# Eight tiles of each down-projection take seven block products instead of seven tiles, and part of the weight sums is made by DMA

## The reference

```
def squared_relu_mlp(n, w_up, w_down):
    return jnp.square(jax.nn.relu(n @ w_up)) @ w_down      # 1024 -> 4096 -> 1024

h = h + squared_relu_mlp(rmsnorm(h, g_ffn[layer]), w_up[layer], w_down[layer])   # layer 0 and 1
```

## Time and profile before

| what | us |
|---|---|
| median of three runs | 946.07 (945.78 to 946.14) |
| profiled execution, device time | 946.75 |
| its span | 944.8 |
| TensorE busy in the span | 935.6 |
| VectorE busy | 712.6 |
| ScalarE busy | 595.3 |
| GpSimd busy | 36.2 |

### The profile page before, as it was taken

How to read it: one execution, slowest core, us unless ns; L and a number is a source line. 1 busy time by engine, 2 the same in 40 slices (tenths; PEclk the granted TensorE clock), 3 DMA queues, 4 the chain that set the end, 5 groups by cost and what they waited for, 6 DMA issues and landing times.

```text
span 944.8 us, 14583 instructions
## 1 busy us (share of the span) xinstructions
PE 935.6 (99%) x5944; PEld 832.5 (88%) x5944; DVE 712.6 (75%) x1037; ACT 595.3 (63%) x869; POOL 36.2 (4%) x15
## 2 busy tenths in 40 slices
PE   8999999999999999999999999999999999999997
PEld 7888888888888888888888888999999999999886
DVE  4997747777988867747777988876468789898643
ACT  7676548888655658838888655734555596555532
POOL 0011250000000000020000000000000000000000
PEclk9999999999999999999999999999999999999999
DMA  8554235555565552535554565454544436555541
GB/s 300 222 183 173 91 134 179 183 200 197 181 220 192 178 209 91 178 136 182 191 207 179 183 218 205 163 191 166 179 165 161 166 134 246 179 179 184 193 158 44
DMA packets 25345, 168.22 MB, mean 178 GB/s; under 512 B 2816, under 2 KB 3904, under 8 KB 5568
## 3 DMA queue, kind: packets, MB, share of 16 engines
q1 hardware_dynamic: 24848, 166.84, 49.5%
q10 hardware_dynamic: 432, 0.46, 0.2%
HBM read 166.24 MB, written 1.05 MB: 177 GB/s over the span
## 4 chain that ended last, share of the span: by engine, by line
PE 94%; DVE 3%; ACT 1%; DMA 1%; issue 1%; SPq 0%; DVEq 0%
PE bank L724 23%; PE bank L725 23%; PE bank L726 23%; PE bank L833 12%; PE bank L837 6%; PE bank L752 1%; DMA raw<-w_stream 1%; DVE wlo L1997 0%; PE bank L887 0%; PE bank L1106 0%; PE bank L891 0%; PE bank L895 0%; PE bank L1240 0%; PE bank L1132 0%; PE bank L1114 0%
## 5 line engine op out<-in xcount | busy, mean ns | idle before, releaser
L1997 DVE TENSOR_TENSOR wlo<-raw,whi 128x2048 fp32r<-128x2048 f32 (+2 forms) x133 | 296.8, 2232 | 131.2 <-ACT whi L1340 131.0
L1340 ACT ACTIVATE whi<-raw 128x2048 fp32r<-128x2048 f32 (+1 forms) x139 | 264.7, 1905 | 100.2 <-PE bank L726 97.7
L833 PE MATMUL bank<-nhl,whi 128*128 128x512 f32 x512 | 124.0, 392 | 0.0
L833 PEld LDWEIGHTS bank<-nhl,whi 128*128 128x128 f32 x512 | 94.0, 188 | 18.8 <-issue 0.7
L724 PE MATMUL bank<-mhi,whi 128*128 128x258 f32 x384 | 108.5, 282 | 0.1
L725 PE MATMUL bank<-mlo,whi 128*128 128x258 f32 x384 | 108.3, 282 | 0.0
L726 PE MATMUL bank<-mhi,wlo 128*128 128x258 f32 x384 | 108.2, 282 | 0.0
L724 PE MATMUL bank<-nhl,whi 128*128 128x258 f32 (+3 forms) x320 | 92.2, 288 | 0.0
L725 PE MATMUL bank<-nhl,whi 128*128 128x258 f32 (+3 forms) x320 | 91.4, 286 | 0.0
L726 PE MATMUL bank<-nhl,wlo 128*128 128x258 f32 (+3 forms) x320 | 90.5, 283 | 0.0
L724 PEld LDWEIGHTS bank<-mhi,whi 128*128 128x128 f32 x384 | 72.5, 189 | 0.4 <-issue 0.2
(11 more groups left out here) (389 smaller groups left out, 1914.3 us busy)
## 6 DMA issues: line engine op xcount, KB each, us to landing
raw<-w_stream SPq DMA_DIRECT2D x154, 1024.0 KB, 4.8
h<-x_rows SPq DMA_DIRECT2D x4, 256.0 KB, 5.1
raw<-w_stream SPq DMA_DIRECT2D x2, 512.0 KB, 6.7
cst<-consts SPq DMA_DIRECT2D x1, 832.0 KB, 6.3
e<-g_post SPq DMA_DIRECT2D x1, 512.0 KB, 6.7
out_rows<-e SPq DMA_DIRECT2D x2, 256.0 KB, 2.0
raw<-w_stream SPq DMA_DIRECT2D x1, 352.0 KB, 10.0
vec<-vectors SPq DMA_DIRECT2D x1, 258.5 KB, 9.5
```

The source lines that it names most:

```text
L833: return pe.matmul(us[c].t[:, :], w[:, k, c * P:c * P + P].hi, nboth[:, k, :], start=k == 0, stop=k == 7)
L1340: act.activation(whi[j][:, 0:n], raw[j][:, 0:n], ACT.Copy).then_inc(s_hi.up(i))
L1997: dve.tensor_tensor(wlo[j][:, 0:m], raw[j][:, 0:m], whi[j][:, 0:m].bitcast(F32), ALU.subtract).then_inc(s_lod.up(i))
```

## The change

SEVEN becomes (2, 4, 5, 7, 8, 10, 11, 13): eight tiles for each layer instead of seven, from tile 4 on two of three. The signs of the scheme change so that the first two of the four weight sums are b12 + b11 and b12 + b22. These two are no longer made by VectorE from `raw`. SP issues two transfers of 256 KB, each of which brings b12 from HBM to one half of a buffer `T13` (`right_block`), and when both have landed, GpSimd issues a transfer of 512 KB that adds b11 and b22 to it (`block_sums`, with `accum_op=ALU.add`). There are two buffers T13, used in turn; the first lies where constants of the first block were, the second where `TX[0]` was. VectorE keeps the other two sums, in `T24`. The tile itself is still brought whole to its slot `raw`.

```diff
-SEVEN = (2, 4, 6, 8, 10, 12, 13)
+SEVEN = (2, 4, 5, 7, 8, 10, 11, 13)
...
-        TX = [at(f"tr{i}", 1024, o_nhl + 4096 * i) for i in range(2)]
+        o_inval = CST["inval"][0]
+        T13 = [cst[:, o_inval:o_inval + 1024], at("tr0", 1024, o_nhl)]
+        T24 = at("tr1", 1024, o_nhl + 4096)
...
+        def fill(l, q):
+            return len(SEVEN[q % 2::2]) * l + q // 2 + 1
+
+        def t13_ready(l, q):
+            return s_t13[q % 2], 16 * fill(l, q)
+
+        def t_sums(l, q):
+            return T13[q % 2], T24
...
             def combined_hi(l, it):
                 q = SEVEN.index(it)
                 for part in range(2):
-                    on.wait_ge(*s_ts.at(l, q, part))
+                    on.wait_ge(*(s_ts.at(l, q) if part else t13_ready(l, q)))
...
             def combined(l, it):
...
                 on.wait_ge(s_raw[i % NSLOT], 16 * (i // NSLOT + 1))
+                on.wait_ge(*t13_ready(l, q))
                 if q:
                     on.wait_ge(*s_tlo.at(l, q - 1, 1))
-                dve.tensor_tensor(TX[0].rearrange("p (k n) -> p k n", k=2), right, above, ALU.subtract).then_inc(s_ts.up(l, q, 0))
-                on.wait_ge(*s_ts.at(l, q, 0))
-                dve.tensor_tensor(TX[1][:, 0:512], r[:, 1536:2048], TX[0][:, 0:512], ALU.subtract).then_inc(own.up())
+                dve.tensor_tensor(T24[:, 0:512], r[:, 1536:2048], t1, ALU.add).then_inc(own.up())
                 on.wait_ge(*own.last())
-                dve.tensor_tensor(TX[1][:, 512:1024], r[:, 1024:1536], TX[1][:, 0:512], ALU.subtract).then_inc(s_ts.up(l, q, 1))
+                dve.tensor_tensor(T24[:, 512:1024], r[:, 1024:1536], T24[:, 0:512], ALU.add).then_inc(s_ts.up(l, q))
...
         def gpsimd_program(pool):
...
+            def block_sums(l, q):
+                t = t_sums(l, q)[0].rearrange("p (k n) -> p k n", k=2)
+                i = DOWN[l] + SEVEN[q]
+                corner = W[starts[i]:starts[i + 1]].rearrange("(p k n) -> p k n", p=P, k=4)[:, 0:4:3, :]
+                on.wait_ge(s_t12[q % 2], 32 * fill(l, q))
+                pool.dma_start(t, corner, accum_op=ALU.add).then_inc(s_t13[q % 2], 16)
+
             for i in range(2, NTILE):
                 j, m, n = i % NSLOT, cuts[i], sizes[i]
+                if seven_at(i):
+                    block_sums(*seven_at(i))
...
+            def right_block(l, q):
+                t = t_sums(l, q)[0].rearrange("p (k n) -> p k n", k=2)
+                i = DOWN[l] + SEVEN[q]
+                b = W[starts[i]:starts[i + 1]].rearrange("(p n) -> p n", p=P)
+                if q < 2:
+                    on.wait_ge(*use["up", l, 15 * q, q].done())
+                else:
+                    on.wait_ge(*s_ts.at(l, q - 2))
+                    on.wait_ge(*s_tlo.at(l, q - 2, 0))
+                for k in range(2):
+                    sp.dma_start(t[:, k, :], b[:, 512:1024]).then_inc(s_t12[q % 2], 16)
...
+                if i - 1 in (DOWN[0] + SEVEN[1], DOWN[1] + SEVEN[1]):
+                    right_block(*seven_at(i - 1))
+                if seven_at(i) and seven_at(i)[1] != 1:
+                    right_block(*seven_at(i))
```

More of the change, by code:

```diff
@@ L586, in block_kernel @@
         ASP = [Pair(at(f"ash{i}", 512, o, F32R), at(f"asl{i}", 512, o + 2048, F32R)).view("p (i n) -> p i n", i=4) for i, o in enumerate(o_sums)]
-        ASP = [ASP + [f.view("p (m n) -> p m n", m=16)[:, 2:10:2, P:2 * P]] for f in FFP]
+        ASP = [ASP + [f.view("p (m n) -> p m n", m=16)[:, m:m + 12:3, P:2 * P] for m in (2, 4)] for f in FFP]
         AS4 = AS.rearrange("p (i n) -> p i n", i=4)
@@ L682, in block_kernel @@
         s_as, s_ashi, s_aslo = (sig(n, grid(2, len(SEVEN))) for n in ("as", "ashi", "aslo"))
-        s_ts, s_thi, s_tlo = (sig(n, grid(2, len(SEVEN), 2)) for n in ("ts", "thi", "tlo"))
+        s_ts = sig("ts", grid(2, len(SEVEN)))
+        s_thi, s_tlo = (sig(n, grid(2, len(SEVEN), 2)) for n in ("thi", "tlo"))
+        s_t12, s_t13 = ([sem(f"s_{n}_{i}") for i in range(2)] for n in ("t12", "t13"))
+        def fill(l, q):
[4 more added lines that the diff above has]
+            return T13[q % 2], T24
         s_ex = sig("ex", range(2))
@@ L1349, in combined_hi @@
                 for part in range(2):
-                    on.wait_ge(*s_ts.at(l, q, part))
+                    on.wait_ge(*(s_ts.at(l, q) if part else t13_ready(l, q)))
                     if q:
                         on.wait_ge(*use["st", l, 3 - part].done(q - 1))
-                    act.activation(TH[part], TX[part], ACT.Copy).then_inc(s_thi.up(l, q, part))
+                    act.activation(TH[part], t_sums(l, q)[part], ACT.Copy).then_inc(s_thi.up(l, q, part))
             def down_hi(l, it):
@@ L2324, in combined @@
                 q, i = SEVEN.index(it), DOWN[l] + it
-                r = raw[i % NSLOT]
-                right, above = r.rearrange("p (k c n) -> p k c n", k=2, c=2)[:, :, 1, :], r[:, 0:1024].rearrange("p (k n) -> p k n", k=2)
+                r, t1 = raw[i % NSLOT], t_sums(l, q)[0][:, 0:512]
                 on.wait_ge(s_raw[i % NSLOT], 16 * (i // NSLOT + 1))
+                on.wait_ge(*t13_ready(l, q))
                 if q:
                     on.wait_ge(*s_tlo.at(l, q - 1, 1))
-                dve.tensor_tensor(TX[0].rearrange("p (k n) -> p k n", k=2), right, above, ALU.subtract).then_inc(s_ts.up(l, q, 0))
-                on.wait_ge(*s_ts.at(l, q, 0))
-                dve.tensor_tensor(TX[1][:, 0:512], r[:, 1536:2048], TX[0][:, 0:512], ALU.subtract).then_inc(own.up())
+                dve.tensor_tensor(T24[:, 0:512], r[:, 1536:2048], t1, ALU.add).then_inc(own.up())
                 on.wait_ge(*own.last())
-                dve.tensor_tensor(TX[1][:, 512:1024], r[:, 1024:1536], TX[1][:, 0:512], ALU.subtract).then_inc(s_ts.up(l, q, 1))
+                dve.tensor_tensor(T24[:, 512:1024], r[:, 1024:1536], T24[:, 0:512], ALU.add).then_inc(s_ts.up(l, q))
             def combined_lo(l, it):
@@ L2341, in combined_lo @@
                     on.wait_ge(*s_thi.at(l, q, part))
-                    dve.tensor_tensor(TL[part], TX[part], TH[part].bitcast(F32), ALU.subtract).then_inc(s_tlo.up(l, q, part))
+                    dve.tensor_tensor(TL[part], t_sums(l, q)[part], TH[part].bitcast(F32), ALU.subtract).then_inc(s_tlo.up(l, q, part))
             def down_lo(l, it):
@@ L2373, in seven_2 @@
                 on.wait_ge(*p7.gone())
-                dve.tensor_tensor(EX[3], EX[1], p5.t[:, :], ALU.add).then_inc(s_ex.up(l))
-                dve.tensor_tensor(EX[0], EX[2], p5.t[:, :], ALU.add).then_inc(p5.free)
+                dve.tensor_tensor(EX[3], p5.t[:, :], EX[1], ALU.subtract).then_inc(s_ex.up(l))
+                dve.tensor_tensor(EX[0], p5.t[:, :], EX[2], ALU.subtract).then_inc(p5.free)
                 on.wait_ge(*s_ex.at(l))
@@ L2398, in row_sums @@
                     on.wait_ge(*s_ffsq.at(l, m))
-                    dve.tensor_tensor(s1, a21, a22, ALU.add).then_inc(own.up())
+                    dve.tensor_tensor(s1, a21, a22, ALU.subtract).then_inc(own.up())
                     on.wait_ge(*own.last())
@@ L2403, in row_sums @@
                     on.wait_ge(own.sem, own.n - 1)
-                    dve.tensor_tensor(s4, a12, s2, ALU.subtract).then_inc(s_as.up(l, q))
+                    dve.tensor_tensor(s4, a12, s2, ALU.add).then_inc(s_as.up(l, q))
                 def row_sums_lo(m):
@@ L2408, in row_sums_lo @@
                     on.wait_ge(*s_ashi.at(l, q))
+                    on.wait_ge(*s_fflo.at(l, m))
                     s = ASP[l][q]
@@ L2869, in stage @@
                         if seven_at(i - NSLOT):
-                            on.wait_ge(*s_ts.at(*seven_at(i - NSLOT), 1))
+                            on.wait_ge(*s_ts.at(*seven_at(i - NSLOT)))
                         if cuts[i - NSLOT]:
```

## The result

| | before | after |
|---|---|---|
| median, us | 946.0 (945.51 to 946.38, 6 runs) | 989.23 (987.78 to 994.53, 6 runs) |
| ratio | | 1.047 (95% interval 1.0454 to 1.0487) |

The account below looks back on a forecast made before the run. TensorE, busy 935.6 of 944.8 us, was taken to bound the kernel. The median 946.07, less 1.36 of matmuls, plus 5.8 of waits on the transfer chain, gave 950.5 us; range 944.3 to 957.3.

Parts of the forecast that it names:

- The direct gain: TensorE in the down-projections: one block product less in each of two layers saves 1.36 us, 0.14%.
- The loop: Tile 8 reuses tile 5's buffer T13, so its sums wait for VectorE's rest, b12 twice and GpSimd's adding transfer.
- C: Time from the rest of tile 5 to the landed sums of tile 8: 10.0 us, ends 7.5 and 14.7.
- limit of 8.2 us: Longest C for tile 11 without a TensorE wait if tile 8 was late: 14.97 - 6.8 = 8.2 us.
- The 8.9 for tile 8: Longest C for tile 8 without a TensorE wait: 14.97 + 2.0 - 6.8 - 1.3 = 8.9 us.
- upper end of 14.7: The high end given for C, the time from tile 5's rest to tile 8's landed sums: 14.7 us.
- b12 twice: SP's two b12 transfers, 512 KB, priced between 64 KB at 2.4 and 1024 KB at 4.8 us: 3.6 us.
- adding transfer behind it: GpSimd's 512 KB adding transfer after its issue: 5.3 us, between 3.5 and 7.1.
- The windows of the other pairs: Time for the chains of other tiles: 11.6 us for tile 5, 11 to 13 us for tiles 7, 10 and 13.
- the forecast's own formula: TensorE's wait per layer is C - 8.9 at tile 8 plus C - 8.2 at tile 11: 2.9 us, 5.8 in two.
- rival 2: DMA engines become the bound, 15.7 to 17.0 us per three tiles if adding costs twice: 958.5 us, chance 0.22.
- Rival 1: The transfer chain is short enough (C at 8.2) that TensorE has no wait: 944.7 us, chance 0.36.

Follow-up runs that it names:

- experiment 4: Kernel before with only the new SEVEN tile numbers; VectorE makes all four weight sums, no transfers added: 947.64 us, ratio 1.0017.
- 12: Changed kernel, but SP issues tiles 5, 8 and 11 only when the same tile's adding transfer has landed: 1007.54 us (one run).
- experiment 8: experiment 4 plus all the change's transfers, in one series from GpSimd's queue into unread buffers, awaited once per layer: 997.65 us, ratio 1.0541.
- experiment 3: Changed kernel with own buffers for the first two sums of tiles 8, 10, 11 and 13: 966.21 us, ratio 1.0219.
- 1: Changed kernel with the adding left out of GpSimd's transfer, which only copies b11 and b22: 969.22 us (one run).
- 9: Changed kernel with tiles 3 to 14 of each down-projection issued as four 256 KB pieces in 2 KB rows: 979.66 us, ratio 1.0361.
- 14: experiment 3 with tiles 3 to 14 of each down-projection issued as four 256 KB pieces in 2 KB rows: 958.22 us, ratio 1.0134.
- experiment 5: Changed kernel, but VectorE makes the first two sums of tiles 5, 8 and 11; the other five tiles use transfers: 986.6 us, ratio 1.0435.

## Why the prediction was wrong

**The direct gain, 1.36 us.** The matmuls went. In experiment 4, where no transfer disturbs, the time still rose by 1.6 us: VectorE has no gap left in that form, with three instructions for the sums of a tile. With the change's two sums the forecast had 13.8 of 14.97 us for VectorE; the durations are in the trace as taken (0.69 each, `tl` 1.22), so nothing speaks against this step, but it never came to decide.

**The loop.** The mechanism is the forecast's: VectorE's first sum waits for GpSimd's transfer, TensorE for what VectorE does behind it, and a round takes C + 6.8 us (6.5 measured behind the wait, 282.20 to 288.70). The rounds bear out its limit of 8.2 us. The 8.9 for tile 8 took tile 5 to be in time, which it was not. TensorE's waits show at the first products of the tile itself, which need its `lo` (the row at 285.50), not at the first matmul on `th`, as `lo` is queued behind the same wait.

**C = 10.0: the term that failed.** Measured 16.5 for tile 8 and 17.3 for tile 11, over even the forecast's upper end of 14.7 for it. The prediction's own sign of being wrong, an adding transfer that lands over 7 us, is what came.

| term | forecast | after (tile 8) | no plain tile beside it (12, tile 8) |
|---|---|---|---|
| SP's wake | 0.1 | 0.07 | |
| b12 twice | 3.6 | 6.1 | 5.9 |
| GpSimd's issue | 1.0 | 1.2 | 1.2 |
| adding transfer behind it | 5.3 | 9.1 | 4.75 |
| C | 10.0 | 16.5 | 11.9 |

Two terms are off, for two reasons. The b12 pair was priced by size, between 64 KB at 2.4 us and 1024 KB at 4.8. But it took 6.1 us in the kernel after, where nothing else moved from 266 to 270 us, and 5.0 at the end of experiment 8: more than a tile of 1 MB. It is two transfers in rows of 2 KB, cut out of rows of 8 KB; which of the two makes it slow, the rows or the number, no run tells. The adding transfer alone was priced well (4.75, and up to 6.0 in the other places of 12, against 5.3); beside the tiles it takes half as much again to twice that. The forecast took the crowd for a part of it only. In fact the two tiles behind `right_block` begin to move when b12 is in, together with it.

**The windows of the other pairs, 11.6 us and more.** They were called safe, and at C = 10 they are. Tile 5's chain took 259.20 - 240.28 = 18.9 us, and that is the 6 us ahead of the first round.

**From C to the time.** Put into the forecast's own formula, 16.5 - 8.9, 17.3 - 8.2 and 18.9 - 11.6 are 24.0 us in a layer, 48.0 in two; with the gain of 1.36, 992.7 us against 989.2. So the formula holds within 3.5 us and its input was wrong. The forecast let C into the time four times (two waits in two layers); with tile 5's wait it is six. The range reached to C = 11.7 only, though the text had 14.7 as the upper end. By that end alone the formula gives 2 x (29.4 - 17.1 + 3.1) = 30.8 and 975.5 us: a range that takes in the bounds of the unknown costs, as it should, would still have missed, by 14 us and not by 32. The range also left out 958.5, the time of its own rival 2, which had a chance of 0.22. A slip without weight: at C = 11.2 the formula gives 955.3, not 955.1.

**Rival 2, the DMA engines.** Its budget (15.7 to 17.0 us for a round) is near the 17.2 from the shares, but in the kernel after, the engines have a share of 0.80 from 252 to 284 us: the loop ends later. With the loop cut they are full (1.03 in experiment 3). Its time of 958.5 is 8 under the 966.2 of experiment 3.

**Rival 1, the chain closes.** Refuted: even with no plain tile beside it a chain took 11.7 to 13.1 us (8 and 12). The estimate from the Trainium skill (DMA: Bandwidth & Descriptors, Anatomy of one DMA), 3.2 us for 512 KB from GpSimd's queue, is under all that was measured: a plain one took 4.3 and 6.8 us (medians of the two buffers in 1), an adding one 5.9 to 7.2 with the engines to itself. No run has a plain one alone. On adding, the rule of the Trainium skill (the same page, Rules for kernel authors: the accumulate reads its destination) agrees with the doubled packets and engine time. That a DMA engine takes its queues in turns by packets (the Trainium skill, the same page, Queues, rings and completion order) agrees in direction with 9 and 14. No run here shows the turns themselves.

**What stays open.** How the 20 us of experiment 3 divide between full engines and turns: the adding is worth 13.9 of them and the small rows 8, which is more than 20 together, so the two overlap. Why b12 twice takes 5 to 6 us alone is open too.

## What to carry to other kernels

A buffer that is refilled by a chain of transfers makes a loop: add up wake, every issue, every landing and the work behind, compare the sum with the time between two uses, and measure one such chain beside the real traffic before work moves to it (VectorE was spared 1.26 us per tile for a chain of 16.5). If a term of the chain is not in the trace, let its upper end into the range, times the number of rounds. Give each refill a buffer of its own, and in an in-order queue issue it ahead of what waits for something else; then look at the budget of the DMA engines, which is the next limit.

## What the runs showed of the hardware

- A transfer of 512 KB that adds takes 3.15 us of all 16 DMA engines, a plain one 1.5; 272 packets against 144; GpSimd's issue 1.20 us against 0.72.
- Two transfers of 256 KB in rows of 2 KB, issued together, landed after 6.1 us from SP's queue (kernel after) and 5.0 from GpSimd's (8) without other traffic, longer than a tile of 1 MB in rows of 8 KB (4.8). While they moved in the kernel after, the DMA engines stood at 0.53 and 113 GB/s.
- With full engines the rate was 415 GB/s from 270 to 275 us of the kernel after and 297 in the 5 us behind, in which most of the adding transfer moved.
- An adding transfer of 512 KB lands after 5.9 to 7.2 us with the engines to itself (8, 12), 10.3 in the kernel after and 13.3 in experiment 5, beside tiles.
- TensorE's granted clock was 1.00 until 282 us, 0.50 from 283 to 289 and 1.00 from 290, around a gap without a matmul from 279.19 to 285.50. At 0.50, matmuls of 128x512 follow each other every 0.43 us in place of 0.23.
